# Seven Strassen products for eight in the feed-forward input projections of a streaming encoder

## The reference, cut to what matters

```python
D_MODEL, D_FF = 1024, 2816

def rms_norm(x, g):
    y = xf * lax.rsqrt(jnp.mean(xf * xf, axis=-1, keepdims=True) + EPS)
    return (y * g.astype(jnp.float32)).astype(x.dtype)

def swiglu(h, w_gate, w_up, w_down):
    return (jax.nn.silu(h @ w_gate) * (h @ w_up)) @ w_down

for layer in range(DEPTH):          # DEPTH = 2
    x = x + 0.5 * swiglu(rms_norm(x, ...), ...)
    x = x + mixer(rms_norm(x, ...))  # layer 0: windowed attention | gated convolution; layer 1: pooling
    x = x + 0.5 * swiglu(rms_norm(x, ...), ...)
```

## Time and profile before

| | us |
|---|---|
| median of 3 runs | 2194.8 |
| lowest, highest run | 2192.29, 2195.33 |
| span of the profiled execution | 2193.0 |

### The profile page before, as it was taken

One profiled execution on the slowest core, in us unless ns is written; L12 is line 12 of the kernel. 1 busy time (PEld: TensorE's weight loads), 2 busy tenths in 40 slices (PEclk: granted clock), 3 DMA queues, 4 the chain that ended last, 5 costly groups with the idle time before them and its releaser, 6 DMA issues. The chain is left out here.

```text
span 2193.0 us, 37242 instructions
## 1 busy us (share of the span) xinstructions
PE 2173.6 (99%) x14778; PEld 2139.6 (98%) x14778; DVE 1008.2 (46%) x1744; ACT 631.6 (29%) x1066; POOL 44.6 (2%) x78
## 2 busy tenths in 40 slices
PE   8999999999999999999999999999999999999998
PEld 6999999999889999999999999999999999999998
DVE  6444434454655543442445443433455643443435
ACT  6212212243434421221224322222224421221223
POOL 5000000001000000000000000000000000000000
PEclk9999999999999999999999999999999999999999
DMA  5332232332212223223223223313222223223302
GB/s 152 91 87 60 75 96 55 80 93 74 59 39 59 78 67 86 77 63 91 77 58 91 58 63 96 96 39 96 79 85 64 58 53 86 77 70 83 96 1 86
DMA packets 311413, 164.02 MB, mean 75 GB/s; under 512 B 14827, under 2 KB 308919, under 8 KB 311336
## 3 DMA queue, kind: packets, MB, share of 16 engines
q1 hardware_dynamic: 308640, 158.36, 26.5%
q0 software_dynamic: 2576, 4.57, 1.0%
q10 hardware_dynamic: 120, 0.04, 0.0%
HBM read 158.94 MB, written 4.00 MB: 74 GB/s over the span
## 5 line engine op out<-in xcount | busy, mean ns | idle before, releaser
L447 PE MATMUL psum<-xg_hi,in_hi 128*128 128x320 f32 x3104 | 966.4, 311 | 1.5 <-DVE xg_lo L1085 1.0
L449 PE MATMUL psum<-xg_hi,in_lo 128*128 128x320 f32 x3104 | 959.8, 309 | 0.0
L448 PE MATMUL psum<-xg_lo,in_hi 128*128 128x320 f32 x3104 | 959.8, 309 | 0.0
L447 PEld LDWEIGHTS psum<-xg_hi,in_hi 128*128 128x128 f32 x3104 | 583.2, 188 | 7.6 <-issue 3.9
L448 PEld LDWEIGHTS psum<-xg_lo,in_hi 128*128 128x128 f32 x3104 | 583.5, 188 | 0.6
L449 PEld LDWEIGHTS psum<-xg_hi,in_lo 128*128 128x128 f32 x3104 | 583.3, 188 | 0.0
L447 PE MATMUL psum<-a_hi,out_hi 128*128 128x320 f32 x1536 | 475.4, 310 | 2.8 <-DVE x L1090 2.0
L449 PE MATMUL psum<-a_hi,out_lo 128*128 128x320 f32 x1536 | 474.6, 309 | 0.0
L448 PE MATMUL psum<-a_lo,out_hi 128*128 128x320 f32 x1536 | 474.6, 309 | 0.0
L1130 DVE TENSOR_TENSOR t<-psum,rstd 128x320 f32<-128x320 f32 x176 | 86.4, 491 | 518.5 <-PE psum L449 511.8
L855 ACT ACTIVATE t<-t 128x320 f32<-128x320 f32 x176 | 83.2, 473 | 795.4 <-DVE t L1130 795.4
(11 more groups left out here) (155 smaller groups left out, 833.0 us busy)
## 6 DMA issues: line engine op xcount, KB each, us to landing
in_raw<-in_ffn_w_gate SPq DMA_DIRECT2D x88, 512.0 KB, 4.0
in_raw<-in_ffn_w_up SPq DMA_DIRECT2D x88, 512.0 KB, 5.3
out_raw<-in_ffn_w_down SPq DMA_DIRECT2D x64, 512.0 KB, 4.1
out_raw<-in_ffn_w_down SPq DMA_DIRECT2D x32, 384.0 KB, 3.4
in_raw<-in_mix_w_in SPq DMA_DIRECT2D x14, 512.0 KB, 5.1
out<-y_nat SPq DMA_DIRECT2D x5, 512.0 KB, 3.2
x_nat<-in_x_prompt SPq DMA_DIRECT2D x4, 512.0 KB, 5.2
in_raw<-in_mix_w_in SPq DMA_DIRECT2D x8, 256.0 KB, 4.7
```

Source lines behind the costliest of these rows:

```text
L447: pe.matmul(dst, w_hi, v_hi, start=first, stop=False)
L448: pe.matmul(dst, w_hi, v_lo, start=False, stop=False)
L449: return pe.matmul(dst, w_lo, v_hi, start=False, stop=last)
```

## The change

The two token halves and the two halves of the width make the normalised activations a 2 x 2 block matrix (B11, B12, B21, B22: first index the width half, second the token half). Gate and up, each in two width halves, make the other 2 x 2 matrix. Of the 22 chunks of a feed-forward the first 4 (PLAIN) are computed as before; for the other 18 the eight block products become seven of 4 k tiles, 12 matmuls each. GROUPS become 4, 6, 6, 6.

- The blocks are normalised in full (gain and rstd) during the first two plain chunks (normalised), their differences T3, T1, T2, T4 during the other two (less). High and low parts: T3 and T2 among the plain units, B11 and B21 after output pair 0 of group 0, T1 and T4 after pair 1, B22 after pair 2, with the weights of the first Strassen chunk after it.
- GpSimd makes three weight sums of 512 columns with four operations per chunk (weight_sums).
- ScalarE copies seven weight slots of 512 columns to in_hi in four operations (weights_early, weights_late), each once the products that read these slots in the chunk before are done; VectorE forms the low parts (fast_lo_split).
- The seven products lie in banks 0, 1, 2, 3, 6, 7 and 5. ScalarE copies the first to SBUF (p1); VectorE adds the others up with seven additions, each of one PSUM bank and one SBUF operand, into gate and up of the two halves (evacuate); silu, product and hidden split stay.
- The next phase's first two weight chunks are split after output pair 0 of the last group.
- The bias_s DMAs move from the start to behind the cache loads. All loops are written out; buffers are laid out anew.

```diff
-GROUPS = (6, 8, 8)
+GROUPS = (4, 6, 6, 6)
+PLAIN = GROUPS[0]
+FAST = FT - PLAIN
...
+        PRODUCTS = ["B11", "B21", "T2", "T3", "T1", "T4", "B22"]
+        PRODUCT_BANK = [0, 1, 2, 3, 6, 7, 5]
+        BLOCKS = ["T3", "T2", "B11", "B21", "T1", "T4", "B22"]
...
+            def part(bank, slot, b):
...
+                for k in range(4):
+                    end = product(psum[:, bank, 0:HALF], w_hi[:, k], w_lo[:, k], hi[:, k], lo[:, k], k == 0, k == 3)
+                end.then_inc(prod_mm, 1)
...
+                for p, (b, bank) in enumerate(zip(PRODUCTS, PRODUCT_BANK)):
+                    if p in (0, 2, 4, 6):
+                        pe.wait_ge(fast_split, 4 * s + p // 2 + 1)
+                    if fresh is not None:
+                        pe.wait_ge(block_lo, 7 * fresh + BLOCKS.index(b) + 1)
+                    if p == 0:
+                        wait(pe, p1_done, s)
+                    elif s > 0:
+                        pe.wait_ge(evac_done, 7 * (s - 1) + (1, 2, 3, 5, 6, 7)[p - 1])
+                    if p == 6:
+                        wait(pe, x_updated, used)
+                    part(bank, p, b)
...
+                            def before_k(k):
+                                if i == 0 and j == 0 and k == 0:
+                                    pe.wait_ge(hidden_lo, hidden - 2 if half == 0 else hidden)
+                                if g and i == 0 and (j, half) == (0, 0) and k == gk - 1:
+                                    pe.wait_ge(hidden_lo, hidden - 1)
+                                if g and i == 0 and (j, half) == (1, 0) and k == 0:
+                                    pe.wait_ge(evac_done, 7 * fast_chunk(index, f0 + gk - 1) + 7)
...
+            def weights_early(index, f):
...
+                act.wait_ge(in_landed[n % 2], landed(n))
+                if not first:
+                    act.wait_ge(prod_mm, 7 * s - 5)
+                fast_hi_split((0, 2), raw_blocks(n % 2, 0, 2))
+                if not first:
+                    act.wait_ge(prod_mm, 7 * s - 3)
+                act.wait_ge(sum_done, 4 * s + 3)
+                fast_hi_split((2, 4), sums[:, 0:2])
+                if not first:
+                    act.wait_ge(prod_mm, 7 * s - 1)
+                fast_hi_split((4, 6), raw_blocks(n % 2, 2, 4))
...
+            def normalised(index, m, made, name, high, half):
+
+                for k in range(4):
+                    last = dve.scalar_tensor_tensor(made[:, k], x[:, 4 * high + k, cols(half)], vec[:, 8 * m + 4 * high + k:8 * m + 4 * high + k + 1],
+                                                    rstd[:, half], ALU.mult, ALU.mult)
+                last.then_inc(block_made, 1)
...
+            def evacuate(to, bank, more, s, p, number):
+
+                dve.wait_ge(prod_mm, 7 * s + p + 1)
+                dve.tensor_tensor(to, psum[:, bank, 0:HALF], more, ALU.add).then_inc(evac_done, 1)
...
+                    for f in range(f0, f0 + gk) if g else ():
+                        s, i = fast_chunk(index, f), f - f0
+                        u = 44 * index + 2 * f
+                        early = weights_early(f + 1) if f + 1 < FT else []
+                        if i > 0:
+                            gate_high(s - 1)
+                            hidden_split(i - 1, 0, u - 1, 1)
+                            hidden_high(s - 1)
+                            weights_late(f)
+                            hidden_split(i - 1, 1, u, 0)
+                        wait(dve, hidden_done, u - 1)
+                        gate_low(s)
+                        ups_begun(s, early[0:1])
+                        ups(s, u, early[1:2])
+                        for split in early[2:3]:
+                            fast_lo_split(*split)
...
+                        if g == 0:
+                            if i == 0:
+                                block_split(index, "B11")
+                                block_split(index, "B21")
+                            elif i == 1:
+                                block_split(index, "T1")
+                                block_split(index, "T4")
+                            elif i == 2:
+                                block_split(index, "B22")
+                                for split in weights_early(PLAIN):
+                                    fast_lo_split(*split)
+                            else:
+                                weights_late(PLAIN)
+                        if g == 3 and i == 0 and after != "end":
+                            c = SPLIT_CHUNK[after]
+                            in_lo_split(IN_CHUNK[after] % 2, c)
+                            in_lo_split((IN_CHUNK[after] + 1) % 2, c + 1)
...
+            def weight_sums(phase, index):
+
+                for f in range(PLAIN, FT):
+                    s, n = fast_chunk(index, f), IN_CHUNK[phase] + f
+                    raw = raw_blocks(n % 2, 0, 4)
+                    pool.wait_ge(in_landed[n % 2], landed(n))
+                    if f == PLAIN:
+                        pool.wait_ge(block_lo, 7 * index + BLOCKS.index("B21") + 1)
+                    wait(pool, fast_split, 4 * s - 2)
+                    pool.tensor_tensor(sums[:, 1], raw[:, 0], raw[:, 2], ALU.subtract).then_inc(sum_done, 1)
+                    pool.wait_ge(sum_done, 4 * s + 1)
+                    pool.tensor_tensor(raw[:, 2], raw[:, 2], raw[:, 3], ALU.add).then_inc(sum_done, 1)
+                    pool.wait_ge(sum_done, 4 * s + 2)
+                    pool.tensor_tensor(sums[:, 0], raw[:, 2], raw[:, 0], ALU.subtract).then_inc(sum_done, 1)
+                    pool.wait_ge(sum_done, 4 * s + 3)
+                    wait(pool, fast_split, 4 * s)
+                    pool.tensor_tensor(sums[:, 2], raw[:, 1], sums[:, 0], ALU.subtract).then_inc(sum_done, 1)
```

More of the change, by code:

```diff
@@ L82, in first_half_count, with landed @@
     return 8 if m in (0, 5) else 14
+def landed(n):
+    return 32 * (n // 2 + 1) + (32 if n >= IN_CHUNK["mix"] + 1 else 0)
 def first_k(phase):
@@ L540, in ffn @@
             def ffn(phase, index):
                 m = NORM[phase]
+                after = AFTER[phase]
+                for pair in range(PLAIN // 2):
+                    for q, (j, half) in enumerate(((0, 0), (1, 0), (0, 1), (1, 1))):
+                        f = 2 * pair + j
+                        if pair == 0 and j == 0 and (index, half) != (0, 0):
+                            xg_ready(m, half)
+                            norm_mean(m, half)
+                        if pair == 0 and index == 3 and q == 1:
+                            pe.wait_ge(x_updated, OUT_UNIT["ffn3"])
+                        in_unit(SPLIT_CHUNK[phase] + f, (IN_CHUNK[phase] + f) % 2, q % 2, IN_UNIT[phase] + 4 * pair + q, half,
+                                turns_between(j) if pair == 0 and index == 0 and not half else None)
@@ L557, in ffn @@
[L557 to L570 removed]
+                    for f in range(f0, f0 + gk) if g else ():
+                        fast_in(fast_chunk(index, f), index if f == PLAIN else None, OUT_UNIT[phase] + 16 * g)
@@ L571, in out_body @@
+                    hidden = 44 * index + 2 * (f0 + gk)
+                    rows = ROWS_NORM.get(NORM[after]) if g == 3 else None
+                    for i in range(4):
+                        for q, (j, half) in enumerate(((0, 0), (1, 0), (0, 1), (1, 1))):
+                            turning = rows is not None and (i, q) == (3, 3)
                             if turning:
@@ L867, in ffn @@
-                    if g == 0:
-                        in_body(0, peeled=True)
-                        with act.Fori(1, gk // 2) as i:
-                            in_body(i)
-                    elif end:
-                        steps(act, gk // 2 - 1, in_body)
-                        in_body(gk // 2 - 1, False)
-                    else:
-                        steps(act, gk // 2, in_body, peel_last=(index == 0 and g == 2))
-                    landed0, per = OUT_LANDED[phase]
-                    rows = ROWS_NORM.get(NORM[after]) if g == 2 else None
@@ L881, in out_body @@
+                    if g:
+                        gate_high(s)
+                        if f + 1 < FT:
+                            weights_late(index, f + 1)
+                        hidden_split(i, 1, 44 * index + 2 * (f0 + gk), 0)
+                    rows = ROWS_NORM.get(NORM[after]) if g == 3 else None
+                    for i in range(4):
                         v = OUT_UNIT[phase] + 16 * g + 4 * i
                         for q in range(4):
-                            if rows is not None and isinstance(i, int) and i == 3 and q == 3:
+                            if rows is not None and (i, q) == (3, 3):
@@ L1160, in out_body @@
+                    if g:
+                        gate_high(s)
+                        hidden_split(i, 0, u + 1, 1)
+                        hidden_high(s)
+                        hidden_split(i, 1, u + 2, 0)
+                        if f + 1 < FT:
+                            weights_late(f + 1)
```

(2 more changed lines are left out.)

535 lines of the change are left out of this document (327 added, 208 removed).

## The result

| | us |
|---|---|
| changed kernel, median of 4 runs (2176.34 to 2188.53) | 2183.6 |
| kernel before, median of 4 runs (2192.29 to 2195.33) | 2194.9 |
| ratio, 95% interval | 0.9948 [0.9926, 0.9970] |
| span of the changed kernel's profiled execution (its own time 2176.34) | 2174.5 |

The account below looks back on a forecast made before the run. TensorE's matmul count times 0.1467 us was taken as the bound: 2193.0 - 126.7 + 25 + 52 + 8 + 3 = 2154 span, so 2156 us as median. Own range 2135 to 2190; 8 in 10 range 2120 to 2210.

Parts of the forecast that it names:

- The price of a matmul: On TensorE, each matmul removed saves 0.1467 us if nobody makes TensorE wait; 864 fewer give -126.7 us.
- Group 0's output units: TensorE, two PSUM banks ahead, idles for x updates while VectorE splits blocks: 13.1 us in each of four feed-forwards, +52.
- group 3: After output pair 0, next-phase weight parts delay x updates 2.7 us past two units, in three feed-forwards: +8 us.
- The group ends: TensorE idles 3.1 us for late hidden low parts at ends of groups 1 and 2, eight times: +25 us.
- The exclusion of the engines: VectorE operations with two SBUF inputs and GpSimd's exclude one another; evacuations from PSUM are free; 2.6 us lost per chunk.
- the second rival: VectorE becomes the bound, with evacuations blocked too or GpSimd's subtractions slower: 14.7 us a chunk, 2273 us; chance 0.19.
- the signs given: Expected in the profile: VectorE's 320-element products near 0.9 us mean, GpSimd's sums 1.2 to 1.3, evacuations staying at 0.49.
- No stall for weights inside a group: Each product's weights are ready over 4 us before their slot is read, so TensorE doesn't wait inside a group.
- loops at nothing: Writing loops out costs nothing, since the mixer is already written out and has no gap.
- the start: Two more normalisations (3.7 us) precede the split of chunk 2's weights, less 0.5 for shorter output weights: +3 us.
- The first rival: GpSimd's sums fall beside evacuations, so blocking costs little: 2131 us, or 2110 with better interleaving in group 0; chance 0.14.
- The whole gain: All helper work on the other engines hides behind TensorE: 2068 us; chance 0.03.

Follow-up runs that it names:

- Experiment 5: Changed kernel with GpSimd's weight sums delayed, plus 14, 6, 10, 14 matmuls that serve nothing in group 0's idle stretches; 2141.7 us, against 2162.4 with the delay alone.
- experiment 7: Also called version 7: changed kernel with four PSUM banks for output units and GpSimd's weight sums delayed past group ends; 2096.8 us, ratio to kernel before 0.9546.
- Experiment 4: Changed kernel with four PSUM banks in turn for output units instead of two, except in group 3's second half; 2129.9 us, ratio to kernel before 0.9696.
- experiment 2: Changed kernel with GpSimd's weight sums for the second chunk of groups 2 and 3 delayed until the previous group's hidden low parts are done; 2162.4 us.
- experiment 3: Changed kernel with GpSimd's sums cut to 8 of 512 columns in all but each feed-forward's first Strassen chunk; 2143.6 us, one run.
- experiment 6: Kernel before with every hardware loop written out as a Python loop, nothing else changed; 2195.4 us, ratio 1.0001.
- experiment 1: Changed kernel with 28, 12, 20, 28 matmuls that serve nothing ahead of the third unit of group 0's output pair steps; 2192.3 us.

## Why the prediction was wrong, point by point

- **The price of a matmul** (0.1467 us, 864 fewer, -126.7) was the step that failed. The count is exact, the price isn't constant: it rests on the sentence that each matmul removed is worth 0.1467 us "as long as nobody makes TensorE wait", and the forecast then priced the waits at their own length alone. Behind a wait of 1.8 to 3.8 us the clock can be the lower one, and the matmuls there cost 0.267 us; the forecast put this at nothing. In the profiled execution the busy time came out 27 us above the forecast, some 19 of it the clock and 6 the edges of the waits. The idle time came out 7 us better than forecast: 2156 + 27 - 7 = 2176, that execution's own time. The median lies 7 us above it, inside the forecast's own range (2135 to 2190), but the gain of 39 had shrunk to 11. Experiment 5 shows the effect by itself, experiment 7 its part in the sum. The forecast read the clock in the mixer alone, where TensorE never idles, and took it for that of all stages. The trace of the kernel before had a stretch of 10 us at the lower level too, in the pooling between ffn2 and ffn3 (the view by stages):

```profile
1676.00:1680.00 4.00, 4.00 (x19) 3.66 (x18) 0.76 (x1) 0.70 (x2) 0.00 (x0) 0.50 0.00 0
```

There it stood behind no wait, so it doesn't give the rule. The changed kernel has the same 10 us there, so it is no part of the difference. The Trainium skill's TensorE: Matmul & The Clock Gate, section "The HAM clock gate", says that an idle TensorE is put back to 1.2 GHz. The changed kernel's trace agrees for the eight waits of 3.8 us, not for the eight of 2.3 to 3.5 us at the group ends; and in this row TensorE had not idled.
- **Group 0's output units, +52, and group 3, +8:** right, 50.4 (with 1.2 put down to output weights) and 7.7 us measured. Experiment 4 shows the two-bank limit as the mechanism: with four banks the waits for x are 1.5 us. It also shows that the bound behind it is VectorE's work, 19 us.
- **The group ends, +25:** right, 24.4, by experiments 2 and 3. In part this is luck: GpSimd's 512-column operation takes 1.28 us alone and not 1.15, and yet the losses per operation were as laid out. What made up for it no run shows.
- **The exclusion of the engines:** right in kind. Evacuations are free of it; the second rival (2273) is out. It works both ways, which the signs given had too small: GpSimd's sums were to take 1.2 to 1.3 us, their four groups have means of 1.34 to 2.04.
- **No stall for weights inside a group; loops at nothing; the start +3:** right (2.4 for the last; experiment 6 for the loops).
- **The first rival** (sums fall beside evacuations) is out: eight waits of 3.05 us were there. The whole gain, 2068, wasn't reached even by version 7, but it was near: 29 us.

That the other three runs' longer time is clock as well rests on their mean clocks alone (0.981 to 0.984); they have no traces.

## What to carry to other kernels

A wait on the engine that sets the time has two prices: its length, and the lower clock behind it. So work that is taken off TensorE must not come back as waits of about 2 us and more; in version 7 no wait under 1.7 us had the lower clock behind it. More PSUM banks between producer and consumer helped most here (experiment 4). Matmuls that serve nothing helped where they fitted into the gap (experiment 5), and cost time where they ran over (experiment 1). Before elementwise work goes to GpSimd, look which of VectorE's two-input operations fall beside it, and whether a short wait can move it to a stage where VectorE has time.

## What the runs showed of the hardware that was not expected

- The lowered clock isn't a fixed function of the wait. In the changed kernel's profile it stood behind two of four waits of 1.83 us and behind none of the eight at group ends, of 2.3 to 3.5 us; in experiment 4 it stood behind all eight of these, in experiment 1 behind seven. Runs of one kernel differ with it: 2176 to 2189 us at mean clocks of 0.987 to 0.981, where version 7 (0.995 to 0.997) stays within about 3 us.
- A float32 matmul of 128 columns that isn't a transpose counts twice in the trace and costs 0.23 us in a row (81.1 us for 352, experiment 1).
- GpSimd takes 1.28 us for a 512-column float32 subtraction that nothing holds up, more than the 1.15 of the straight ratio to its 0.72 for 320 columns. The changed kernel's timeline in group 0 of ffn3:

```profile
1779.96 1.28 POOL L1627 TENSOR_TENSOR sums<-in_raw 128x512 f32<-128x512 f32 x1
```
